# Expert stage of a two-block transformer kernel: half the early gather, the second pair's rows taken from the packed table, packing moved, last two products swapped

## The reference

```python
gp = softmax(h @ rg_w + rg_b); g_w, g_idx = top_k(gp, 1)            # one of 4 groups
el = (h @ re_w + re_b).reshape(N, 4, 8)[own group]
e_w, e_idx = top_k(softmax(el), 2)                                  # two experts of that group
e_w = g_w * e_w / sum(e_w)
for e in range(32):                                                 # h: 256 tokens x 1024
    he = silu(h @ w_gate[e]) * (h @ w_up[e])                        # w_gate, w_up: 1024 x 256
    y = y + comb[:, e:e+1] * (he @ w_down[e])                       # w_down: 256 x 1024
out = rms_norm(x + y, final_norm_g)
```

## Time and profile before

| | |
|---|---|
| median of 3 executions | 1361.62 us (1361.47 to 1362.68) |
| span of the profiled execution, first to last instruction | 1360.3 us |
| TensorE busy in the span | 1288.3 us (95%) |
| VectorE busy | 906.2 us (67%) |
| ScalarE busy | 586.8 us (43%) |
| GpSimd busy | 52.5 us (4%) |
| mean granted TensorE clock | 0.982 |
| DMA traffic | 289.71 MB, mean 213 GB/s |

### The profile page before, as it was taken

One profiled execution on the slowest core, in us unless ns is written; L12 is line 12 of the kernel. 1 busy time (PEld: TensorE's weight loads), 2 busy tenths in 40 slices (PEclk: granted clock), 3 DMA queues, 4 the chain that ended last, 5 costly groups with the idle time before them and its releaser, 6 DMA issues.

```text
span 1360.3 us, 21695 instructions
## 1 busy us (share of the span) xinstructions
PE 1288.3 (95%) x8713; PEld 1091.2 (80%) x8713; DVE 906.2 (67%) x1469; ACT 586.8 (43%) x917; POOL 52.5 (4%) x82
## 2 busy tenths in 40 slices
PE   7999999989999899999998999969989979999996
PEld 6999999878888799989987888859889966555553
DVE  3999877875555779997687655575786772222223
ACT  3345675444444434566644444444545343111111
POOL 1000000000000000000000000011013000010000
PEclk9999999989999899999998999999999989999999
DMA  9764434465555456443465555555445676999995
GB/s 291 243 195 151 156 98 155 156 216 185 185 185 189 151 184 204 150 148 114 118 215 170 188 192 190 187 178 167 146 137 199 219 290 260 421 421 421 421 420 205
DMA packets 172584, 289.71 MB, mean 213 GB/s; under 512 B 10388, under 2 KB 143140, under 8 KB 160204
## 3 DMA queue, kind: packets, MB, share of 16 engines
q1 hardware_dynamic: 169580, 281.55, 59.2%
q0 software_dynamic: 2752, 6.82, 1.8%
q10 hardware_dynamic: 160, 0.08, 0.0%
HBM read 287.36 MB, written 3.16 MB: 214 GB/s over the span
## 4 chain that ended last, share of the span: by engine, by line
PE 63%; DVE 25%; ACT 5%; DMA 3%; issue 3%; SPq 1%; DVEq 0%; ACTq 0%
PE ps L1823 10%; PE ps L1825 10%; PE ps L1824 10%; DVE w_lo L1159 8%; PE ps L1874 8%; PE ps L2320 7%; DVE cvh L1282 5%; PE ps L1876 4%; ACT w_hi L736 3%; PE ps L2352 3%; DMA raw<-in_w_up 2%; PE ps L2363 2%; DVE nm L1239 1%; DVE gT L1199 1%; DVE x_nat L1205 1%
## 5 line engine op out<-in xcount | busy, mean ns | idle before, releaser
L1159 DVE TENSOR_TENSOR w_lo<-raw,w_hi 128x2048 fp32r<-128x2048 f32 (+1 forms) x165 | 367.1, 2225 | 143.8 <-ACT w_hi L736 143.6
L736 ACT ACTIVATE w_hi<-raw 128x2048 fp32r<-128x2048 f32 (+1 forms) x165 | 307.4, 1863 | 228.5 <-PE ps L1825 213.6
L1823 PE MATMUL ps<-xT_both,w_lo 128*128 128x256 f32 x680 | 197.6, 291 | 0.1
L1824 PE MATMUL ps<-xT_both,w_hi 128*128 128x256 f32 x680 | 192.9, 284 | 0.0
L1825 PE MATMUL ps<-xT_both,w_hi 128*128 128x256 f32 x680 | 192.8, 284 | 0.0
L1874 PE MATMUL ps<-xT_both,w_hi 128*128 128x512 f32 x496 | 175.8, 399 | 0.0
L1823 PE MATMUL ps<-w_hi,xT_both 128*128 128x256 f32 (+2 forms) x536 | 161.9, 302 | 1.9 <-DVE w_lo L1159 1.6
L1824 PE MATMUL ps<-w_lo,xT_both 128*128 128x256 f32 (+2 forms) x536 | 159.1, 297 | 0.0
L1825 PE MATMUL ps<-w_hi,xT_both 128*128 128x256 f32 (+2 forms) x536 | 159.1, 297 | 0.0
L1823 PEld LDWEIGHTS ps<-xT_both,w_lo 128*128 128x128 f32 x680 | 130.8, 192 | 3.1 <-issue 2.5
L1824 PEld LDWEIGHTS ps<-xT_both,w_hi 128*128 128x128 f32 x680 | 131.0, 193 | 0.2
(11 more groups left out here) (412 smaller groups left out, 2259.1 us busy)
## 6 DMA issues: line engine op xcount, KB each, us to landing
raw<-in_w_in SPq DMA_DIRECT2D x72, 1024.0 KB, 5.1
raw<-in_w_ff SPq DMA_DIRECT2D x64, 1024.0 KB, 5.3
raw<-in_w_down SPq DMA_DIRECT2D x10, 1024.0 KB, 15.7
raw<-in_w_up SPq DMA_DIRECT2D x10, 1024.0 KB, 17.2
w_exp<-in_w_down SPq DMA_DIRECT2D x10, 1024.0 KB, 17.3
raw<-in_w_o SPq DMA_DIRECT2D x8, 1024.0 KB, 4.9
w_exp<-in_w_gate SPq DMA_DIRECT2D x8, 1024.0 KB, 16.6
raw<-in_w_gate SPq DMA_DIRECT2D x8, 1024.0 KB, 17.4
```

The lines of the kernel that those rows point to most:

```text
L736: nc.scalar.activation(split_of(u)[0][:, 0:n], raw[:, u % RAW, 0:n], ACT.Copy).then_inc(hi_done, 1)
L1159: nc.vector.tensor_tensor(split_of(u)[1][:, 0:n], raw[:, u % RAW, 0:n], split_of(u)[0][:, 0:n].bitcast(F32), ALU.subtract).then_inc(split_ ...
L1823: nc.tensor.matmul(out_, left[1], right[0], start=start, stop=False)
L1824: nc.tensor.matmul(out_, left[0], right[1], start=False, stop=False)
```

## The change

Four things are done to the first round of the expert stage:

1. The early gather makes only pair 0's 128 slot columns; its 32 matmuls are 128 columns wide where they were 256. Pair 1's slot rows are copied by GpSimd from `packed`, as for the later pairs.
2. All eight packs come after `inner(0, 1)`; both `place_slots` come ahead of it.
3. `outer(0)` is done ahead of `inner(1, 0)`, so the first duos in `FIRST` are (0,0), (0,1), (0,2), (1,0), (1,1).
4. `inner(15, 1)` comes ahead of `outer(14)`, with the loads in the same order, and `turn_he(15)` ahead of `scatter(14)`. ScalarE's tanh and VectorE's swish of pair 15 are moved ahead of pair 14's output work to match.

```diff
-FIRST = [(0, 0), (0, 1)] + [x for p in range(PAIRS - 1) for x in ((p + 1, 0), (p, 2), (p + 1, 1))] + [(PAIRS - 1, 2)]
+FIRST = [(0, 0), (0, 1), (0, 2), (1, 0), (1, 1)] + [x for p in range(1, PAIRS - 2) for x in ((p + 1, 0), (p, 2), (p + 1, 1))] + [(PAIRS - 1, 0), (PAIRS - 1, 1), (PAIRS - 2, 2), (PAIRS - 1, 2)]
...
+        def width(r):
+
+            return 2 * CAP if r is None else T
...
-            for p in range(2, PAIRS):
+            for p in range(1, PAIRS):
                 at = [pool.value_load(base_i[0:1, 2 * p + e:2 * p + e + 1], min_val=0, max_val=BANK - CAP) for e in range(2)]
-                if p == 2:
+                if p == 1:
                     pool.wait_ge(gath_c, 4 + KC)
-                pool.wait_ge(duo_used, duo_at(None, p - 2, 1) + 1)
+                else:
+                    pool.wait_ge(duo_used, duo_at(None, p - 2, 1) + 1)
...
-                if r is None:
-                    for k in range(4):
-                        pack_copy(k)
...
                 for p in range(PAIRS):
-                    q = p % 2
-                    act.wait_ge(duo_used, plus(duo_at(r, p, 1) + 1, DUOS))
-                    nc.scalar.activation(eg[:, q, :], gate_up(r, p)[:, 0:T], ACT.Tanh, scale=0.5).then_inc(th_done, 1)
+                    if r is not None or p < PAIRS - 1:
+                        tanh_half(p)
                     if r is None and p == 0:
-                        for k in range(4, KC):
+                        for k in range(KC):
                             pack_copy(k)
...
-                                last = nc.tensor.matmul(ps[:, gather_bank(r, n), c * T:(c + 1) * T], x[:, a, k * P:(k + 1) * P], picks[:, a, quad % 2],
+                                last = nc.tensor.matmul(ps[:, gather_bank(r, n), c * T:c * T + width(r)], x[:, a, k * P:(k + 1) * P], picks[:, a, quad % 2, 0:width(r) // CAP],
...
-                    if r is None and kind == 0 and p >= 2:
-                        pe.wait_ge(slots_put, p - 1)
+                    if r is None and kind == 0 and p:
+                        pe.wait_ge(slots_put, p)
...
                     inner(0, 0)
-                    for k in range(4):
-                        pack(k)
                     place_slots(0)
                     place_slots(1)
                     inner(0, 1)
-                    for k in range(4, KC):
+                    for k in range(KC):
                         pack(k)
-                    for p in range(PAIRS):
-                        if p >= 1:
-                            if p + 1 < PAIRS:
-                                place_slots(p + 1)
-                            inner(p, 1)
+                    turn_he(0)
+                    outer(0)
+                    inner(1, 0)
+                    for p in range(1, PAIRS):
+                        if p + 1 < PAIRS:
+                            place_slots(p + 1)
+                        inner(p, 1)
+                        if p < PAIRS - 1:
                             scatter(p - 1)
-                        turn_he(p)
-                        if p + 1 < PAIRS:
+                            turn_he(p)
                             inner(p + 1, 0)
-                        outer(p)
+                        else:
+                            outer(p - 1)
+                            turn_he(p)
+                            scatter(p - 1)
+                        if p != PAIRS - 2:
+                            outer(p)
```

More of the change, by code:

```diff
@@ L1073, in gather_copy @@
                         k = 2 * j + c
-                        last = nc.scalar.activation(xg_chunk(quad, k), bank[:, c, :], ACT.Copy, scale=gain_slot[:, k:k + 1])
+                        last = nc.scalar.activation(xg_chunk(quad, k)[:, 0:width(r)], bank[:, c, 0:width(r)], ACT.Copy, scale=gain_slot[:, k:k + 1])
                     last.then_inc(gath_c, 1)
@@ L1085, in moe_round, with tanh_half @@
                     gather_copy(n)
-                if r is None:
-                    for k in range(4):
-                        pack_copy(k)
+                def tanh_half(p):
+                    act.wait_ge(duo_used, plus(duo_at(r, p, 1) + 1, DUOS))
+                    nc.scalar.activation(eg[:, p % 2, :], gate_up(r, p)[:, 0:T], ACT.Tanh, scale=0.5).then_inc(th_done, 1)
                 for p in range(PAIRS):
-                    q = p % 2
-                    act.wait_ge(duo_used, plus(duo_at(r, p, 1) + 1, DUOS))
-                    nc.scalar.activation(eg[:, q, :], gate_up(r, p)[:, 0:T], ACT.Tanh, scale=0.5).then_inc(th_done, 1)
+                    if r is not None or p < PAIRS - 1:
+                        tanh_half(p)
                     if r is None and p == 0:
-                        for k in range(4, KC):
+                        for k in range(KC):
                             pack_copy(k)
@@ L1101, in moe_round @@
                         gather_copy(5 + 2 * p)
+                    if r is None and p == PAIRS - 2:
+                        tanh_half(PAIRS - 1)
                     for h in range(2):
@@ L1752, in moe_round @@
                             place_slots(p + 1)
-                        swish(p)
+                        if p < PAIRS - 1:
+                            swish(p)
                         if p % 2 == 0 and p + 2 < PAIRS:
@@ L1756, in moe_round @@
                             weigh_picks(p // 2 + 1)
+                        if p == PAIRS - 2:
+                            swish(PAIRS - 1)
                         low_sums(p)
```

## The result

The changed kernel takes 1365.70 us (median of 8), the one before 1362.53 us in the same comparison: a ratio of 1.0026, 95% interval 1.0017 to 1.0035. It is slower by 3.2 us in the medians and by 0.26% in the ratio, which is 3.5 us (2.3 to 4.8). I had forecast no change, 1362.1 us, with 9% for a slowdown of this size.

A forecast was written before the change was run, and what follows sets the result against it. The weight-load stream, gapless from load 9 once duo 2 is free, was taken to bound the kernel. Terms 0.96 + 0.03 - 0.1 = +0.9 us, less 0.4 at the end, gave +0.5 us: 1362.1 us, range 1360.2 to 1364.2.

The forecast's parts named there:

- the first term of the sum: Early gather: halving the columns of its 32 matmuls taken as 0, between 3.1 us less and 0.9 us more.
- a clock still at 0.50 at 1126: TensorE's clock after the early gather: listed as one of three profile findings that would make the forecast wrong.
- Rival B: Early gather and `inner(0,0)`: clock rises later, costing 0.65 and 2.5 us; 1365.3 us, 0.27% slower; chance 9%.
- Rival A: Early gather: costs by its columns, takes 3.4 us, net 2.0 us earlier, 1360.1 us; chance 8%.
- The anchor: Start of the gapless load stream: load 9 waits until duo 2 is free, then all later loads follow; +0.9 us.
- Moving the packs: Packing behind `inner(0,1)`: load 8 issued at about 1132.3, worth 0 because load 9 still waits for duo 2.
- My sum of 39 loads: Weight stream, loads 9 to 47: 39 x 4.99 = 194.6 us from about 1145.0, giving 1339.6.
- The wait for `heT`: `outer(0)` starts 1.27 us after `turn_he(0)`, behind ScalarE's copy, 0.96 us later than `inner(1,0)` did.
- One change from product to pack less: Start of the expert stage: one change from `inner` to pack falls away, -0.1 us.
- The swap at the end: End of the expert stage: `outer(15)` starts 6.1 us after load 46 arrives instead of 6.46, -0.4 us.
- GpSimd's slots for pair 1: Two copies, 1.16 us, ending at 1142.0 and needed at 1144.6: cost 0, with 2.6 us of cover.
- Rival C: Lag at load 9's release is not there; only the end's -0.4 is left, 1361.2 us; chance 8%.

The follow-up runs named there:

- the fastest version: Kernel before plus all packs behind pair 0's down product, extra matmuls ahead of the 256-wide gather, swap at the end: 1358.46 us (0.9963), again 1359.00 us (0.9978).

## Why the prediction was wrong

**The step that failed** is the first term of the sum: "So the weight load sets the spacing, and halving the columns buys about nothing: I take 0", with 0.9 us more as its far end. The spacing at the low clock was right: 7.00 us for 32 matmuls is 0.219 us each, as the 32-column ones had said. What I left out of the sum is that the clock, which rose inside the wide gather, doesn't rise in the narrow one. It costs 0.82 us in the gather and 2.21 us in the first product, 3.0 us in all. The run with the wide gather gave those 3.0 us back; the run with the narrow gather alone brought them in the old order. One of my signs of being wrong, "a clock still at 0.50 at 1126", is what the windows show. What it is in the narrow matmuls that leaves the clock low, no run here shows.

**Rival B was this mechanism**, with 9%: its terms were 0.65 and 2.5 us, a rise at 1130 and 1365.3 us; measured were 0.82 and 2.21 us, 1129.2 and 1365.7 us. My ground for holding it small, that "the engine has work without a pause from 1118.3 on", was the wrong measure. It had work without a pause in both kernels, and only the wide one got its clock. No row of before showed a gather this thin followed by a rise, so nothing in the rows held the chance as low as one in ten. Rival A, a gather that costs by its columns, fell: 0.219 us per matmul at 128 columns.

**The anchor** held. Load 9's issue moved by +3.87 us against the mark of the gather's start and the arrival of load 46 followed it to 0.1 us. Moving the packs was forecast at 0, with load 8 about 3.8 us earlier, and the run with that and the swap gave 1.0001 and 3.8 us. The forecast spoke of the release of duo 2 as "the anchor of the whole stage"; the run with the packing last showed that this holds only while no later load starts behind a gap. My sum of 39 loads was read loosely: it gives 1339.6 for the end of load 47, and "some 5 us after s" further on is 1343.2. The trace of before has the last piece of load 47 landing at 1343.1, with a DMA share of only 0.13 from 1340 to 1344: the stream thins out at its end, and 1339.6 is about where that begins. Nothing in the forecast hung on it.

**The wait for `heT`**: +0.96 forecast, +0.99 measured, and 1.0 between the two runs that differ in it. **One change from product to pack less**: -0.1 forecast, -0.19 measured with the packs in one piece. **The swap at the end**: -0.36 worked out (rounded to -0.4), -0.26 measured. VectorE's `y_lo` ended 5.02 us after the start of `outer(14)`, as forecast; from there to `outer(15)` it is 1.18 us where I had 1.04. **GpSimd's slots for pair 1** cost nothing, as forecast: `inner(1,0)` has no wait in the trace. Rival C, no lag, is out.

Put together with the clock in it, 0.9 + 3.0 - 0.3 = +3.6 us at the end of the stage, within the interval of the measurement (+2.3 to +4.8 us).

The Trainium skill ("TensorE: Matmul & The Clock Gate", section "What's actually happening") says that the clock is set by how busy the array has been recently. The traces agree: without the extra matmuls the clock is at 0.50 behind the wait of 4.5 us, with them it stays at 1.00. They also show that work without a pause is not by itself enough, since both gathers run without one and the clock rises only in the wide one.

## What to carry to other kernels

Before making a matmul narrower, see what sets its spacing and at what clock it runs: if each has its own weight load, fewer columns save almost nothing, and behind an idle stretch they can leave the clock low for the work that follows. In a stage that is fed by a ring of buffers, work out for each load when its buffer comes free plus the time of all loads from it on; only the largest of these sums is worth shortening, and an earlier release elsewhere just moves the gap. A product put directly behind the transposes that feed it pays the copy between them; keep an independent product there.

## What the runs showed that I had not expected

Work that nobody reads makes this kernel faster. 47 extra matmuls in TensorE's waits take the gather from 6.18 to 3.99 us.

There is a wait far ahead of the change with two lengths. In the second block, TensorE's transposes wait for VectorE's `qkT` for either 1.6 or 2.8 us. Eight of the twelve traces have the short one. The four with the long one all have the extra matmuls, but one trace with them has the short one: in the fastest version the first trace has the short wait,

```profile
1021.02 0.44 PE L457 MATMUL ps<-ident,qkT 128*128 128x128 f32 x2 [1.61 <-DVE qkT L1461]
```

and the second trace, of the same kernel, the long one:

```profile
1020.94 0.44 PE L457 MATMUL ps<-ident,qkT 128*128 128x128 f32 x2 [2.79 <-DVE qkT L1461]
```

The wait ends at the same time in both, so it isn't what shifts the program. What differs is where a stretch of low clock falls. In the first trace it lies ahead of the wait: TensorE gets there about 1.2 us later and waits that much less.

```profile
1012.00:1014.00 2.00, 2.00 (x11) 2.00 (x11) 1.97 (x4) 0.58 (x2) 1.71 (x1) 0.50 0.28 66
```

In the second trace the clock is 1.00 in that window, and the low stretch lies behind the wait, where nothing hides it:

```profile
1022.00:1024.00 2.00, 2.00 (x9) 1.41 (x5) 1.91 (x1) 2.00 (x9) 1.98 (x2) 0.50 0.28 55
```

By 1026 the second trace is 1.5 us behind the first, and it stays so up to the gather; their spans are 1357.5 and 1358.9 us. The other traces fall in line: the low stretch is ahead of the wait in all eight with the short one and behind it in all four with the long one. It can be why the extra matmuls in the kernel before showed 1.5 us in the ratio where the trace, read from the mark, shows 2.0; how often an execution without a trace has the one or the other isn't known. What decides on which side the low stretch falls stays open; the extra matmuls are issued some 90 to 100 us after it. For effects below 2 us it was the reading from a mark inside the trace that told more than the medians.
